# Three edge norms of a diffusion trunk: sums of squares by one product with a matrix of ones, square root and reciprocal over all tokens

## What is computed

```python
def rmsnorm(x, w):
    y = x * lax.rsqrt(jnp.mean(x * x, axis=-1, keepdims=True) + EPS)
    return y * w

for i in range(DEPTH):                       # 2 layers
    hx = rmsnorm(x, norm_mix[i]) * (1.0 + sc1) + sh1      # the same for ctx
    ox, oc = mixer_i(hx, hc)
    x = x + g1 * ox
    x = x + g2 * swiglu(rmsnorm(x, norm_ffn[i]) * (1.0 + sc2) + sh2, ffn_w_in[i], ffn_w_out[i])
return rmsnorm(x, norm_final)
```

## Time and profile before

| | |
|---|---|
| median of 3 runs | 1624.17 us (1623.48 to 1624.51) |
| the profiled execution | 1622.78 us |
| its span, first to last instruction | 1621.1 us |
| PE busy | 1585.7 us (98% of the span) |
| DVE busy | 963.1 us (59%) |
| ACT busy | 594.5 us (37%) |
| granted clock of PE, mean | 0.994 of full speed |
| share of PE in the chain that ended last | 88% |

### The profile page before, as it was taken

How to read it: one execution, slowest core, us unless ns; L and a number is a source line. 1 busy time by engine, 2 the same in 40 slices (tenths; PEclk the granted TensorE clock), 3 DMA queues, 4 the chain that set the end, 5 groups by cost and what they waited for, 6 DMA issues and landing times.

```text
span 1621.1 us, 23708 instructions
## 1 busy us (share of the span) xinstructions
PE 1585.7 (98%) x9248; PEld 1352.7 (83%) x9248; DVE 963.1 (59%) x1620; ACT 594.5 (37%) x860; POOL 99.9 (6%) x95
## 2 busy tenths in 40 slices
PE   7999999999999999999999999989999999999998
PEld 5889988888888888888888889877778888888886
DVE  5665436635486767767767765888856533333334
ACT  4334447633342211222112224667744431222222
POOL 0000000000000000000000000046630000000003
PEclk8999999999999999999999999999999999999999
DMA  9342310013234334344334413320002323332332
GB/s 335 113 130 65 99 46 26 27 52 105 79 89 134 115 130 129 104 129 129 123 118 123 130 59 111 106 77 2 1 27 78 104 82 100 104 99 82 104 91 92
DMA packets 197311, 156.07 MB, mean 96 GB/s; under 512 B 6690, under 2 KB 194254, under 8 KB 197230
## 3 DMA queue, kind: packets, MB, share of 16 engines
q1 hardware_dynamic: 197230, 154.97, 31.2%
HBM read 149.71 MB, written 2.10 MB: 94 GB/s over the span
## 4 chain that ended last, share of the span: by engine, by line
PE 88%; ACT 4%; DVE 4%; issue 1%; DMA 1%; SPq 1%; DVEq 0%; ACTq 0%
PE ps L597 86%; PE ps L1135 1%; ACT pr L1709 1%; DVE w_lo L1755 1%; DMA ada_pre<-in_w_ada 1%; DVE scaled L1809 1%; DVE h_lo L1818 1%; ACT w_hi L1250 1%; PE ps L1140 1%; SPq L397 0%; DVE row_max L2402 0%; ACT h_hi L1309 0%; DMA w_raw<-in_ffn_w_out 0%; PE ps L913 0%; ACT pT L1684 0%
## 5 line engine op out<-in xcount | busy, mean ns | idle before, releaser
L597 PE MATMUL ps<-h_hi,w_hi 128*128 128x512 f32 (+1 forms) x1392 | 497.0, 357 | 1.5 <-DVE w_lo L1755 1.5
L597 PE MATMUL ps<-h_lo,w_hi 128*128 128x512 f32 (+1 forms) x1392 | 490.2, 352 | 0.0
L597 PE MATMUL ps<-h_hi,w_lo 128*128 128x512 f32 (+1 forms) x1392 | 490.2, 352 | 0.0
L1755 DVE TENSOR_TENSOR w_lo<-w_raw,w_hi 128x2048 fp32r<-128x2048 f32 (+1 forms) x88 | 197.2, 2240 | 196.2 <-ACT w_hi L1250 196.1
L597 PEld LDWEIGHTS ps<-h_hi,w_hi 128*128 128x128 f32 x1392 | 263.5, 189 | 45.1 <-issue 7.9
L597 PEld LDWEIGHTS ps<-h_lo,w_hi 128*128 128x128 f32 x1392 | 263.6, 189 | 36.6
L597 PEld LDWEIGHTS ps<-h_hi,w_lo 128*128 128x128 f32 x1392 | 263.3, 189 | 36.2
L1250 ACT ACTIVATE w_hi<-w_raw 128x2048 fp32r<-128x2048 f32 (+1 forms) x88 | 165.1, 1876 | 343.6 <-DMA w_raw<-in_ffn_w_in 188.9
L597 PE MATMUL ps<-a_hi,w_hi 128*128 128x512 f32 (+1 forms) x528 | 187.1, 354 | 0.2 <-DVE w_lo L1755 0.2
L597 PE MATMUL ps<-a_lo,w_hi 128*128 128x512 f32 (+1 forms) x528 | 186.9, 354 | 0.0
L597 PE MATMUL ps<-a_hi,w_lo 128*128 128x512 f32 (+1 forms) x528 | 186.8, 354 | 0.0
(11 more groups left out here) (263 smaller groups left out, 2055.9 us busy)
## 6 DMA issues: line engine op xcount, KB each, us to landing
w_raw<-in_ffn_w_in SPq DMA_DIRECT2D x88, 512.0 KB, 4.9
ada_w<-in_w_ada SPq DMA_DIRECT2D x41, 1024.0 KB, 5.2
w_raw<-in_ffn_w_out SPq DMA_DIRECT2D x32, 512.0 KB, 3.9
w_raw<-in_gla_w_in SPq DMA_DIRECT2D x24, 512.0 KB, 4.8
ada_pre<-in_w_ada SPq DMA_DIRECT2D x7, 1024.0 KB, 11.6
w_raw<-in_ffn_w_out SPq DMA_DIRECT2D x16, 384.0 KB, 3.7
w_raw<-in_gla_w_o SPq DMA_DIRECT2D x8, 512.0 KB, 6.4
w_raw<-in_swa_w_o SPq DMA_DIRECT2D x8, 512.0 KB, 4.5
```

The lines of the kernel that those rows point to most:

```text
L597: return pe.matmul(o, w, r, start=start, stop=stop, skip_group_check=skip)
L1755: dve.tensor_tensor(w_lo[s][:, 0:kc, :], raw_of(n)[:, 0:kc, :], w_hi[s][:, 0:kc, :].bitcast(F32), ALU.subtract).then_inc(wlo_ok, 1)
```

## The change

`first_slab` no longer calls `statistics` and `spread`. At k = 3 it calls a new helper, `totals`: a product with the whole 128 x 128 matrix of ones as weights and `ssq` as moving data, 512 columns and 256 columns (only the 512 on edge 2). That leaves the sum over the partitions on every partition at once, in `S67`. ACT takes the root of all of `S67` and writes `rb` (`deviations`), and DVE replaces `rb` by its reciprocal in place (`inverses`). DVE's `normal` waits for a new semaphore, `rbi_ok`, that the reciprocal raises, in place of `rbs_ok`, which now means the root; PE at k = 6 still waits for `rbs_ok`. The other norms keep the old form; their semaphore counts change.

```diff
+        def totals(m, segs):
+
+            pe.wait_ge(ssq_ok, m)
+            for sg in reversed(segs):
+                last = mm(S67[:, sg[0]:sg[1]], ones[:, :], ssq[:, sg[0]:sg[1]], True, True)
+            last.then_inc(ss_done, 1)
+
...
-                    statistics(m, tiles)
-                if k == 4:
-                    spread(m, tiles)
+                    totals(m, segs)
                 if k == 6:
...
-        def spread_out(m, a):
-
-            act.wait_ge(bc_done, m + 1)
-            act.activation(rb[:, a:T], S67[:, a:T], ACT.Copy).then_inc(rbs_ok, 1)
+        def deviations(m, a):
+
+            act.wait_ge(ss_done, m + 1)
+            act.activation(rb[:, a:T], S67[:, a:T], ACT.Sqrt, bias=eps_t[:, 0:1], scale=1.0 / D).then_inc(rbs_ok, 1)
...
-                deviation(5 + 2 * l, D, a // P)
-                spread_out(5 + 2 * l, a)
+                deviations(5 + 2 * l, a)
...
-        deviation(6, D)
-        spread_out(6, 0)
+        deviations(6, 0)
...
+        def inverses(e, a):
+
+            dve.wait_ge(rbs_ok, e + 1)
+            dve.reciprocal(rb[:, a:T], rb[:, a:T]).then_inc(rbi_ok, 1)
...
             if c0 == 0:
-                dve.wait_ge(rbs_ok, e + 1)
+                dve.wait_ge(rbi_ok, e + 1)
...
-                inverse(m, a // P)
+                inverses(2 * l, a)
...
-        inverse(6)
+        inverses(KV_EDGE, 0)
```

More of the change, by code:

```diff
@@ L233, in trunk @@
     rh_ok, rl_ok, kf_done, sh_ok, rbs_ok, bz_ok = sems("rh_ok", "rl_ok", "kf_done", "sh_ok", "rbs_ok", "bz_ok")
-    zg_ok, zp_ok, zk_ok = sems("zg_ok", "zp_ok", "zk_ok")
+    zg_ok, zp_ok, zk_ok, rbi_ok = sems("zg_ok", "zp_ok", "zk_ok", "rbi_ok")
     bw_done, br_ok, ua_ok = sems("bw_done", "br_ok", "ua_ok")
@@ L798, in first_slab @@
             stats_no[0] += 1
-            tiles = range(TILES) if len(segs) == 2 else range(2, TILES)
             pe.wait_ge(wlo_ok, n + 1)
@@ L1238, in _ @@
         result((0, 1, 2), (6, 7)).then_inc(yt_done, 1)
-        pe.wait_ge(std_ok, stats_no[0] + 1)
+        pe.wait_ge(std_ok, 6)
         result((3,), range(4, DC)).then_inc(yt_done, 1)
@@ L1275, in deviation @@
         def deviation(m, n_elems, t0=0, b=6):
-            act.wait_ge(ss_done, m + 1)
+            act.wait_ge(ss_done, m + 1 + 3 * int(m == 5))
             act.activation(std[:, t0:TILES], bank(b, 8 + t0, TILES - t0), ACT.Sqrt, bias=eps_t[:, 0:1],
@@ L1739, in _ @@
         ffn(1, F1, (LAT,))
-        deviation(8, D, 2)
+        deviation(5, D, 2)
         for t in range(4):
-            act.wait_ge(rs_ok, 9)
+            act.wait_ge(rs_ok, 6)
             act.wait_ge(yt_done, 1 + t // 3)
@@ L2468, in _ @@
         ffn(1, 7, F1, (LAT,))
-        dve.wait_ge(std_ok, 9)
+        dve.wait_ge(std_ok, 6)
         dve.reciprocal(rstd[:, 2:TILES], std[:, 2:TILES]).then_inc(rs_ok, 1)
-        dve.wait_ge(rs_ok, 9)
+        dve.wait_ge(rs_ok, 6)
         for t in range(4):
```

## The result

| | before | after |
|---|---|---|
| median, device us | 1624.11 (20 runs, 1622.48 to 1625.55) | 1626.10 (20 runs, 1624.91 to 1628.74) |
| ratio to before, 95% interval | | 1.0014 (1.0008 to 1.0020) |
| span of the profiled execution | 1621.1 | 1625.5 |
| PE busy | 1585.7 | 1582.8 |
| DVE busy | 963.1 | 975.8 |

What follows compares the result with a forecast made beforehand. PE bounds the kernel, but at each edge the later of PE's products and DVE's chain from `rb` counts. Delays of +0.27, +0.17 and +1.02, say 1.5 us, on 1624.2 gave 1625.7 us, range 1621.2 to 1631.2.

Steps and rivals of the forecast that it cites:

- sum of +1.46: Later starts of the next bound piece: +0.27 us at edge 0, +0.17 at edge 1, +1.02 at edge 2.
- part 1: PE at the edges: long products replace sums and spreading, saving 1.04, 1.04 and 0.56 us, 2.64 in all.
- part 2: ACT's wide root: starts 0.17 us behind the product, takes 912 ns on 768 columns, 687 ns on 512.
- part 3: DVE's wide reciprocal at 5.7 ns a column: 4.54 us for 768 columns, 3.08 us for 512.
- part 4: Start of DVE's chain behind each edge: 0.27 us later at edge 0, 0.44 at edge 1, 1.02 at edge 2.
- Edge 1: Chain starts 0.44 us later; DVE's 0.27 us transfer wait takes up its part, leaving +0.17 when attention starts.
- tie of two paths: At attention's start, PE's first scores end about when DVE takes up the first maximum, at 1068.22 us.
- Rival 1: DVE's reciprocal takes about 8.4 ns a column, 6.61 us for 768: +7.0 us, 1631.2 us; chance 0.20.
- Rival 2: DVE's reciprocal streams like a plain pass, 0.96 us for 768 columns: -4.1 us, 1620.1 us; chance 0.08.
- Rival 3: Idle stretches between edge and third slab absorb the late chain; PE's 2.64 us come through, 1621.5 us; chance 0.12.
- What would show it: Trace signs: reciprocal 4.5 and 3.1 us; PE idle before third slabs 2.4 us (edge 0), 2.0 (edge 2).
- signs of being wrong: PE's waits not growing with a rightly priced reciprocal, or a place without a wait today starting to wait for `h_lo`.

Runs made afterwards that it cites:

- e1_plain: The changed kernel with the wide reciprocal of rb replaced by a plain DVE pass of the same width, norms left out: 1618.98 us, 0.9968 of before.
- e2_twice: The changed kernel with each edge's wide reciprocal done twice, the first into a scratch row nobody reads: 1640.98 us, 1.0105 of before.

## Why the prediction was right, step by step

The forecast was 1625.7 us with a sum of +1.46; measured were 1626.1 and +2.0. The cause was the one named: PE's saving turned into waiting, and the chain that the reciprocal stands in set the ends at edges 0 and 2 as worked out. At edge 1 the number came out by luck: what takes the delay up there is not what the prediction named. The terms of the sum were off by some tenths of a microsecond. The prediction called a difference of 0.1% no difference, since a measurement could tell 0.2%; with 20 runs of each kernel 0.12% could be told.

- **PE's products (part 1).** The two long products moved the next start by 1.10 us and the one after that by 0.42 where 0.23 is usual (440.55, 440.97 against 439.45), 1.29 in all, for which 1.48 had been taken. Counted in the same way at edge 2, 512 columns cost 0.86, two thirds of it, so there is no fixed gap of 0.2; and sums and spreading cost 1.34 each where 1.26 had been read. So PE saved 1.39 us at edge 0 (1.42 by the floors), and by the floors of the experiments 1.43 at edge 1 and 0.97 at edge 2, and not 1.04, 1.04 and 0.56. It changed nothing, since PE waited.
- **ACT's root (part 2)** took 903 and 690 ns for 912 and 687 taken, and began 1.49 us behind the sums for 1.65 worked out. The next product started 0.38 earlier than taken, but the root followed it by 0.39 and not by 0.17.
- **The reciprocal (part 3)** was under-sized: 5.7 ns a column were taken, the middle of 5.2 and 6.3, and 6.25 was measured. That is +0.41 us at edges 0 and 1 and +0.27 at edge 2. The reading from one to four columns was right, by luck, since a single instruction stood behind it; that from one to six was too low. A difference of 26 ns, in readings that scatter by 13 and 15, was drawn out from 5 columns to 767.
- **The chain's start (part 4).** At edge 0 the idle 1.05 us went, as forecast, and `h_lo` began 0.52 later, not 0.27: +0.41 for the reciprocal, -0.17 for the earlier root. A further 0.20 was not foreseen. Before, ACT made the two pieces of `h_hi` right behind each other, and DVE went from the first `h_lo` to the second without a wait in any row; now `h_hi` follows `scaled` piece by piece, and DVE waits 0.33 for the second one. The next `w_lo` starts 10.02 us behind the sums (449.47 - 439.45) where it was 9.30, by this row of the timeline before, and from there all of the chain is 0.72 late. At edge 2 +1.15 was measured for +1.02.

```profile
447.05 2.29 DVE L1755 TENSOR_TENSOR w_lo<-w_raw,w_hi 128x2048 fp32r<-128x2048 f32 x1
```

- **Edge 1** came out at +0.16 for +0.17, and that is luck. The first `h_hi` began 0.77 later and not 0.44, so by the prediction's way of counting 0.50 should have been left. The 0.27 that it meant to spend are still there, as 0.29. What was missed is that PE takes up DVE's chain at edge 1 in the same place as at the other edges, at the third slab behind the edge. Before, no wait showed there, because `w_lo` was ready 0.76 us before PE came (1031.68 + 2.29 against 1034.73). DVE and PE before:

```profile
1031.68 2.29 DVE L1755 TENSOR_TENSOR w_lo<-ada_w,w_hi 128x2048 fp32r<-128x2048 f32 x1 [0.16 <-DVE vT L2325]
...
1034.15 0.82 PE L1081 MATMUL ps<-ident,vT 128*128 128x128 f32 x6
1034.73 0.47 PE L597 MATMUL ps<-h_hi,w_hi 128*128 128x512 f32 x1
```

and after, where the sums stand 2.42 us later in the profile:

```profile
1034.89 2.29 DVE L1757 TENSOR_TENSOR w_lo<-ada_w,w_hi 128x2048 fp32r<-128x2048 f32 x1 [0.16 <-DVE vT L2332]
...
1036.09 0.88 PE L1085 MATMUL ps<-ident,vT 128*128 128x128 f32 x6 [0.75 <-ACT vT L1612]
1037.24 0.50 PE L597 MATMUL ps<-h_hi,w_hi 128*128 128x512 f32 x1 [0.27 <-DVE w_lo L1757]
...
1069.40 0.69 DVE L2299 TENSOR_TENSOR q_sw<-q_sw,sinT 128x512 f32<-128x512 f32 x1 [0.29 <-DMA q_sw<-q_rot]
```

The chain brings `w_lo` 0.79 us later (1034.89 - 1031.68 - 2.42), which the 0.76 us of slack take up but for 0.03. PE, with its list 1.43 us shorter, now waits there, first 0.75 us for `vT` and then 0.27 for `w_lo`, and starts the slab 0.09 later than before (1037.24 - 1034.73 - 2.42). From this product to the first scores of attention PE runs through its list, 32.74 us before, 32.81 after and 32.75 in e1_plain and e2_twice, and the end follows the scores at the same distance, 0.74 or 0.75 us, in all of them. So edge 1 is no tie of two paths at its end. It is a wait for DVE's chain as at edges 0 and 2, behind a slack of 0.76 us that the change just used up. DVE itself loses all but 0.07 of its 0.76 us where it had waited 0.60 us for a transfer that hangs on PE's products (at 1050.82 before); that wait is gone after.

- **Rival 1** (8.4 ns a column) falls by the row of 4.95 us, which would have been 6.61. The page of the Trainium skill that spoke for it, "VectorE: DVE Perf Modes" in its section on the 8-slice pipeline, is right that the reciprocal is no plain pass; its repeat count of 8 does not give the price here. By the 0.96 GHz that the Trainium skill gives ("Trainium Kernel Development and Optimization", NeuronCore Architecture; named in the prediction), 6.25 ns would be an estimated 6 cycles a column.
- **Rival 2** (a plain pass) falls by the same row. What it says of the rest is right: with the plain pass of e1_plain the kernel is 5.4 us faster than before, where -4.1 was worked out. By the edges it is 5.9 us. The 1.8 us between this and the 4.1 are PE's larger saving (0.38 + 0.39 + 0.41 us) and waiting before the change that had no row (0.44 us at edge 0, 0.16 at edge 2). Why the medians show 0.5 us less than the edges is open.
- **Rival 3** (the delay is taken up) falls at edges 0 and 2 by their own lengths, and in e2_twice the chain passes an added delay on at all three edges, to within 0.1 us. At edge 1 0.76 us of delay were taken up, though not by idle stretches of the chain but by the time for which `w_lo` had lain ready, and PE's saving did not come through there either.
- **What would show it:** PE's idle time before the third slab was to be 2.4 us at edge 0 and 2.0 at edge 2. It is 3.0 and 1.96 in all, but spread. At edge 0 only 1.07 of it stands at the third slab, with the rest at two earlier places, one of them `h_lo` inside the second slab (1.51 us). At edge 2 it is two waits for `w_lo`:

```profile
1260.49 0.50 PE L597 MATMUL ps<-h_hi,w_hi 128*128 128x512 f32 x1 [0.57 <-DVE w_lo L1757]
...
1273.49 0.49 PE L597 MATMUL ps<-h_hi,w_hi 128*128 128x512 f32 x1 [1.39 <-DVE w_lo L1757]
```

So what the prediction named among the signs of being wrong does show, places that no wait showed before and that now wait: the second slab behind edge 0 for `h_lo`, the second behind edge 2 for `w_lo`, and the third behind edge 1. At edges 0 and 2 it did not make the sum wrong, since the waits hang on one chain, and only where this chain ends counts. At edge 1 it is the step that was missed.

## What to carry to other kernels

Look for slack where the busiest engine takes up the chain, also at places where no wait shows yet: there it is the time for which the data lay ready. Price an edit first on the engine that already sets the next start, here DVE behind each edge, and give the busiest engine's saving nothing until that engine is shown not to wait. A function that is applied to a few columns is cheap at nearly any price a column; moved behind a broadcast it is applied to all of them, so its slope has to be known and not guessed from small shapes. When such a chain is late, look for work that does not depend on it and can fill the idle time ahead of it, and for an idle engine that can do the expensive step: here both together turned a loss of 2.0 us into a gain of 5.2.

## What the runs showed of the hardware

- DVE's reciprocal in f32 takes 152 ns + 6.25 ns a column (4.95 us for 768, 3.35 us for 512), some nine times the 0.56 us in which DVE passes a multiply and add over the same 768 columns. In a second instruction directly behind the first it is 4.90.
- ACT's Ln on 768 columns from PSUM takes 0.90 us and its Exp on 768 columns from SBUF 0.85 us; a load of a function table takes 1.28 us. The load and the Exp, which take the reciprocal's place on the path, are 2.13 us, less than half of it.
- An f32 product of 512 and 256 columns with a full matrix of weights costs PE 1.29 us of its list. Twelve PE instructions of one column each, with a weight load for each, cost 1.34, and the twelve of the spreading, with 128 columns each, cost the same 1.34: here the number of instructions counts and not the columns.
- Behind a stop of PE of 5.24 us (edge 0 of e2_twice) and of 4.57 us (edge 1) the granted clock was 0.50 for a while: a product of 512 columns was followed by the next after 0.43 us where 0.23 is usual, and at edge 1 PE lost 3.08 us. Behind the stops of up to 1.51 us in after, the clock stayed at 1.00.
